# Two blocks over eight experts: the modulation row summed in four column groups, routing by scaled one-hots and bf16 counts, and one remainder moved ahead of the gate

## The reference

```python
# first block, mixture of experts
logits = (t @ w_router).astype(F32)
top_val, top_idx = lax.top_k(logits, TOP_K)          # TOP_K = 2, 8 experts
top_w = jax.nn.softmax(top_val, axis=-1)
combine = jnp.sum(jax.nn.one_hot(top_idx, N_EXPERTS, dtype=F32) * top_w[..., None], axis=1)
for e in range(N_EXPERTS):
    gt, up = jnp.split(t @ w_gate_up[e], 2, axis=-1)
    y = (jax.nn.silu(gt) * up) @ w_down[e]
    out = out + combine[:, e:e + 1].astype(t.dtype) * y
# second block, modulation row: (1, 1024) @ (1024, 6144)
ada = jax.nn.silu(c) @ w_ada[l] + b_ada[l]
shift_a, scale_a, gate_a, shift_m, scale_m, gate_m = jnp.split(ada, N_ADA, axis=-1)
```

## Time and profile before

| | |
|---|---|
| median of 3 runs | 1829.18 us (1827.13 to 1836.05) |
| the profiled execution | 1839.49 us, span 1837.7 us |
| mean granted TensorE clock | 0.981 |
| TensorE busy | 1782.2 us, 97% of the span |
| VectorE busy | 1412.2 us, 77% |
| ScalarE busy | 1113.0 us, 61% |
| GpSimd busy | 118.0 us, 6% |

### The profile page before, as it was taken

One profiled execution on the slowest core, in us unless ns is written; L12 is line 12 of the kernel. 1 busy time (PEld: TensorE's weight loads), 2 busy tenths in 40 slices (PEclk: granted clock), 3 DMA queues, 4 the chain that ended last, 5 costly groups with the idle time before them and its releaser, 6 DMA issues.

```text
span 1837.7 us, 22263 instructions
## 1 busy us (share of the span) xinstructions
PE 1782.2 (97%) x8380; PEld 1456.7 (79%) x8388; DVE 1412.2 (77%) x1225; ACT 1113.0 (61%) x1023; POOL 118.0 (6%) x147
## 2 busy tenths in 40 slices
PE   7979999999999999999999999999999989999998
PEld 6867788778777888888888888888888857778886
DVE  5556787858758888888888888888888976475556
ACT  5653444443537777777777777777777755543333
POOL 3010111112110000000000000000001010000000
PEclk9979999999999999999999999999999999999999
DMA  9536899744159999999999999999999984535550
GB/s 321 196 126 200 271 330 324 270 142 159 36 183 337 377 376 390 379 381 380 380 382 381 375 392 377 386 368 375 384 367 389 394 299 160 149 115 200 188 185 23
DMA packets 237227, 525.94 MB, mean 286 GB/s; under 512 B 16874, under 2 KB 40618, under 8 KB 236992
## 3 DMA queue, kind: packets, MB, share of 16 engines
q1 hardware_dynamic: 223376, 477.23, 72.2%
q0 software_dynamic: 13744, 47.32, 7.7%
HBM read 513.95 MB, written 10.53 MB: 285 GB/s over the span
## 4 chain that ended last, share of the span: by engine, by line
PE 91%; DVE 4%; ACT 2%; DMA 1%; issue 1%; DVEq 0%; SPq 0%; ACTq 0%
PE bank L2752 27%; PE bank L2753 27%; PE bank L2760 27%; PE bank L3192 1%; ACT w_hi L1029 1%; PE bank L2902 1%; DVE w_lo L1644 1%; PE bank L2864 1%; DMA raw<-in_moe_w_down 1%; DMA raw<-in_a_w_mem_kv 1%; PE bank L2808 1%; PE bank L2815 1%; PE bank L3074 0%; PE bank L3551 0%; PE bank L2854 0%
## 5 line engine op out<-in xcount | busy, mean ns | idle before, releaser
L1644 DVE TENSOR_TENSOR w_lo<-raw,w_hi 128x2048 fp32r<-128x2048 f32 x453 | 1040.6, 2300 | 224.4 <-ACT w_hi L1029 210.0
L1029 ACT ACTIVATE w_hi<-raw 128x2048 fp32r<-128x2048 f32 x453 | 867.2, 1916 | 480.3 <-PE bank L2753 341.4
L2752 PE MATMUL bank<-w_hi,slot_hi 128*128 128x512 f32 x896 | 357.1, 399 | 2.6 <-ACT w_hi L1029 2.6
L2753 PE MATMUL bank<-w_hi,slot_lo 128*128 128x512 f32 x896 | 351.0, 392 | 0.0
L2752 PE MATMUL bank<-w_hi,hT_hi 128*128 128x512 f32 (+1 forms) x704 | 279.2, 397 | 5.5 <-ACT w_hi L1029 3.2
L2753 PE MATMUL bank<-w_hi,hT_lo 128*128 128x512 f32 (+1 forms) x704 | 274.2, 390 | 0.0
L2760 PE MATMUL bank<-w_lo,slot_hi 128*128 128x512 f32 x896 | 240.6, 390 | 1.1 <-DVE w_lo L1644 1.1
L2752 PEld LDWEIGHTS bank<-w_hi,slot_hi 128*128 128x128 f32 x896 | 169.4, 189 | 36.6 <-issue 3.0
L2760 PEld LDWEIGHTS bank<-w_lo,slot_hi 128*128 128x128 f32 x896 | 168.1, 188 | 38.1 <-DVE w_lo L1644 2.8
L2753 PEld LDWEIGHTS bank<-w_hi,slot_lo 128*128 128x128 f32 x896 | 169.5, 189 | 33.5
L2760 PE MATMUL bank<-w_lo,hT_hi 128*128 128x512 f32 (+1 forms) x704 | 175.2, 391 | 0.0
(11 more groups left out here) (421 smaller groups left out, 1458.7 us busy)
## 6 DMA issues: line engine op xcount, KB each, us to landing
raw<-in_moe_w_gate_up SPq DMA_DIRECT2D x448, 512.0 KB, 5.9
raw<-in_moe_w_down SPq DMA_DIRECT2D x224, 512.0 KB, 5.8
raw<-in_w_ff SPq DMA_DIRECT2D x64, 512.0 KB, 4.4
work<-in_w_ada POOLq DMA_DIRECT2D x48, 512.0 KB, 5.5
raw<-in_dense_w_gate_up SPq DMA_DIRECT2D x44, 512.0 KB, 5.1
raw<-in_b_w_in SPq DMA_DIRECT2D x24, 512.0 KB, 5.1
raw<-in_w_in SPq DMA_DIRECT2D x24, 512.0 KB, 4.9
raw<-in_dense_w_down SPq DMA_DIRECT2D x22, 512.0 KB, 4.7
```

The source lines that it names most:

```text
L1029: act.activation(w_hi[:, g % SPLIT, 0:n], raw[:, g % RING, 0:n], ACT.Copy).then_inc(R.hi, 1)
L1644: dve.tensor_tensor(w_lo[:, g % SPLIT, 0:n], raw[:, g % RING, 0:n], f32(w_hi[:, g % SPLIT, 0:n]), ALU.subtract).then_inc(R.lo, 1)
L2752: pe.matmul(out_, hi, w_hi[:, s, c:c + w], start=(start and n == 0), stop=False, skip_group_check=True)
L2753: mm = pe.matmul(out_, lo, w_hi[:, s, c:c + w], start=False, stop=False, skip_group_check=True)
```

## The change

The twelve sums of the modulation row go to four groups of 32 columns: sum j fills partitions 32 (j mod 4) on, and three turns replace twelve rows. Four are made before `turn_first` and eight behind the first unit of `b_in`. The row's place is widened to all partitions, cleared by POOL, loaded with the bias in four transfers and stored in four. In the routing, POOL makes x times gain into `mix`, and the norm's scale moves into the one-hots of expert 0; ScalarE makes the scaled h for `h_dram` in `y_rows`. The marks of the chosen, the triangle, the ones, the token numbers and the one-hots of the seven other experts are bf16. ScalarE makes `w_hi` of the fifth unit ahead of the first Silu, VectorE its `w_lo` ahead of the first hidden product, and `route_rest` moves from ahead of the first step of `pair` to its end. The sizes of `one_row` and of a filler buffer (`even`) change with it; waits for the store count four transfers.

```diff
--- before.py
+++ after.py
@@ -59,6 +59,8 @@
 N_ADA = 6
+QUADS = 4
+ADA_TURNS = 2 * N_ADA // QUADS
 ADA_BUFFERS = 3
...
@@ -187,9 +189,10 @@
         zero = sb("zero", [P, P], BF16)
-        ones = sb("ones", [P, P])
+        exact = sb("exact", [P, 2 * P], BF16)
+        later_bf, ones_bf = exact[:, 0:P], exact[:, P:2 * P]
         c_col = sb("c_col", [P, KC])
-        one_row = sb("one_row", [P, 4 * N_ADA - 1])
+        one_row = sb("one_row", [P, 32 + ADA_TURNS - 1])
         sumsq = sb("sumsq", [P, TILES])
...
@@ -597,6 +602,7 @@
         pick = taken_a
+        pick_bf = [taken_a[:, t, P:P + (EXPERTS - 1) * P // 2].bitcast(BF16) for t in range(TILES)]
         h_again = rows[:, :, :]
...
@@ -662,7 +668,15 @@
-            return work[0:2 * N_ADA, 9216:9728]
+            return work[:, 9216:9728]
+
+        def ada_rows_of(quad):
+
+            return work[32 * quad:32 * quad + ADA_TURNS, 9216:9728]
+
+        def by_quad(rows):
+
+            return rows.rearrange("(r q) n -> q r n", q=QUADS)
...
@@ -674,14 +688,19 @@
             pool.wait_ge(*at("mix_a"))
-            pool.dma_start(ada_place(), A["b_ada_2"].rearrange("l (a n) -> (l a) n", n=512)).then_inc(ada_bias_in, 16)
+            pool.memset(ada_place(), 0.0).then_inc(ada_cleared, 1)
+            pool.wait_ge(ada_cleared, 1)
+            for quad in range(QUADS):
+                pool.dma_start(ada_rows_of(quad), by_quad(A["b_ada_2"].rearrange("l (a n) -> (l a) n", n=512))[quad])\
+                    .then_inc(ada_bias_in, 16)
             for n in range(ADA_ROWS):
...
             pool.wait_ge(*at("ada", "row"))
-            pool.dma_start(ada_dram, ada_place()).then_inc(ada_stored, 16)
+            for quad in range(QUADS):
+                pool.dma_start(by_quad(ada_dram)[quad], ada_rows_of(quad)).then_inc(ada_stored, 16)
...
@@ -916,8 +935,14 @@
                 load_gain()
+                pool.wait_ge(gain_in[0], 32)
+                pool.wait_ge(*at("b_out", "added", 1))
+                for t in range(TILES):
+                    o = pool.tensor_tensor(mix[:, t, :], x[:, t, :], gain[:, 0, :], ALU.mult)
+                o.then_inc(S("moe", "gained"), 1)
+                S.also("gain used", 2)
                 pool.wait_ge(*at("norm_moe", "h"))
-                pool.dma_start(h_dram.rearrange("(t p) d -> p t d", p=P), mix[:, :, :]).then_inc(h_stored, 16)
+                pool.dma_start(h_dram.rearrange("(t p) d -> p t d", p=P), y_rows[:, :, :]).then_inc(h_stored, 16)
             if have("ada"):
...
@@ -1293,7 +1318,7 @@
                     if j == 1 and have("ada"):
-                        act.wait_ge(ada_stored, 16)
+                        act.wait_ge(ada_stored, 16 * QUADS)
                     for h in range(2):
...
@@ -1339,10 +1364,14 @@
                 gained(2)
-                squares("moe", x, mix[:, 0, :], at("b_out", "added", 1))
+                squares("moe", x, y_rows[:, 0, :], at("b_out", "added", 1))
                 deviation("moe")
...
                 act.activation(ratio[:, 1, :], ratio[:, 0, :], ACT.Exp).then_inc(S("route", "exp"), 1)
+                act.wait_ge(*at("moe", "gained"))
+                for t in range(TILES):
+                    h = act.activation(y_rows[:, t, :], mix[:, t, :], ACT.Copy, scale=scale_col("moe", t))
+                h.then_inc(S("norm_moe", "h"), 1)
             if have("experts"):
...
@@ -1397,8 +1426,8 @@
                         split_hi(R, g + 3, 0)
+                        split_hi(R, FIRST_STEP, 0)
                         silu(0, g + 3, 0, 1)
-                        split_hi(R, FIRST_STEP, 0)
                         split_hi(R, FIRST_STEP + 1, 0)
...
@@ -1974,6 +2003,11 @@
                         dve.wait_ge(loaded["con"], 16)
+                        dve.tensor_copy(later_bf, con[:, C_LATER:C_LATER + P])
+                        for t in range(TILES):
+                            number = C_DIST + (TILES - 1 - t) * SEQ
+                            o = dve.tensor_copy(token_bf[:, t:t + 1], con[:, number:number + 1])
+                        o.then_inc(S("exact numbers"), 1)
                     if j in (2, 3):
...
@@ -2052,9 +2086,9 @@
                 if have("ada"):
-                    dve.wait_ge(ada_bias_in, 16)
+                    dve.wait_ge(ada_bias_in, 16 * QUADS)
                     dve.wait_ge(*at("ada", "summed"))
-                    dve.tensor_tensor(ada_place(), ada_place(), bank[2][0:2 * N_ADA, :], ALU.add).then_inc(S("ada", "row"), 1)
+                    dve.tensor_tensor(ada_place(), ada_place(), bank[2][:, :], ALU.add).then_inc(S("ada", "row"), 1)
...
@@ -2179,15 +2213,9 @@
                 dve.wait_ge(*S.last())
-                dve.tensor_scalar(chosen[:, :, :], rank[:, :, :], 1.5, None, ALU.is_lt).then_inc(S("route", "chosen"), 1)
+                dve.tensor_scalar(chosen[:, :, 0:EXPERTS], rank[:, :, :], 1.5, None, ALU.is_lt).then_inc(S("route", "chosen"), 1)
                 dve.tensor_scalar(seats[:, :, :], rank[:, :, :], 1.5, 1000.0, ALU.is_gt, ALU.mult).then_inc(S(), 1)
                 dve.wait_ge(*S.last())
-                g = gain_row(2)
-                for t in range(TILES):
-                    h = dve.scalar_tensor_tensor(out=mix[:, t, :], in0=x[:, t, :], scalar=scale_col("moe", t), in1=g,
-                                                 op0=ALU.mult, op1=ALU.mult)
-                h.then_inc(S("norm_moe", "h"), 1)
-                S.also("gain used", 2)
                 dve.wait_ge(*at("route", "order"))
...
@@ -2265,7 +2293,11 @@
                         for t in range(TILES):
-                            o = dve.tensor_scalar(pick[:, t, 0:P], iota, place[:, again, t, bass.ds(e, 1)], None, ALU.is_equal)
+                            if again:
+                                o = dve.tensor_scalar(pick[:, t, 0:P], iota, place[:, 1, t, bass.ds(e, 1)], None, ALU.is_equal)
+                            else:
+                                o = dve.tensor_scalar(pick[:, t, 0:P], iota, place[:, 0, t, e:e + 1], scale_col("moe", t),
+                                                      ALU.is_equal, ALU.mult)
                         o.then_inc(L.picked, 1)
...
@@ -2280,7 +2312,7 @@
                         for t in range(TILES):
-                            o = dve.tensor_tensor(pick[:, t, P:EXPERTS * P].rearrange("p (e s) -> p e s", e=EXPERTS - 1),
+                            o = dve.tensor_tensor(pick_bf[t].rearrange("p (e s) -> p e s", e=EXPERTS - 1),
                                                   iota.unsqueeze(1).broadcast_to([P, EXPERTS - 1, P]),
...
@@ -2296,15 +2328,16 @@
                         split_lo(R, g + 3, 0)
+                        split_lo(R, FIRST_STEP, 0)
                         hidden(0, 1)
-                        route_rest()
...
                             p, half, step = j % 2, j // EXPERT_STEPS, j % EXPERT_STEPS
-                            split_lo(R, g, r)
+                            if again or d > 0 or j > 0:
+                                split_lo(R, g, r)
                             if last and j == PAIR_STEPS - 1:
...
@@ -2323,6 +2356,8 @@
                             hidden(1 - p, n + 1)
+                            if not again and d == 0 and j == 0:
+                                route_rest()
                             if last and j == 8 and not again:
...
@@ -3071,8 +3106,10 @@
                     for j in range(first, last):
-                        mm = pe.matmul(bank[2][0:2 * N_ADA, :], one_row[:, 2 * N_ADA - 1 - j:4 * N_ADA - 1 - j],
-                                       work[:, j * 512:(j + 1) * 512], start=(j == 0), stop=(j == 2 * N_ADA - 1), skip_group_check=True)
+                        quad, turn_ = j % QUADS, j // QUADS
+                        mm = pe.matmul(bank[2][32 * quad:32 * quad + 32, :], one_row[:, ADA_TURNS - 1 - turn_:ADA_TURNS + 31 - turn_],
+                                       work[:, j * 512:(j + 1) * 512], start=(turn_ == 0), stop=(turn_ == ADA_TURNS - 1),
+                                       skip_group_check=True)
                     if last == 2 * N_ADA:
...
@@ -3088,10 +3125,8 @@
                     pe.wait_ge(ada_ready, ADA_ROWS)
-                    sum_ada(0, 2)
+                    sum_ada(0, QUADS)
                 turn_first()
-                if have("ada"):
-                    sum_ada(2, 4)
...
@@ -3118,7 +3153,7 @@
                         if (j, h) == (0, 0) and have("ada"):
-                            sum_ada(4, 2 * N_ADA)
+                            sum_ada(QUADS, 2 * N_ADA)
                         inside(j, h)
...
@@ -3171,10 +3206,10 @@
                 pe.wait_ge(*at("zero"))
-                later = con[:, C_LATER:C_LATER + P]
-                for c, terms in enumerate((((later, 0),), ((ones[:, :], 0), (later, 1)), ((ones[:, :], 0), (ones[:, :], 1)))):
+                pe.wait_ge(*at("exact numbers"))
+                for c, terms in enumerate((((later_bf, 0),), ((ones_bf, 0), (later_bf, 1)), ((ones_bf, 0), (ones_bf, 1)))):
```

(7 more changed lines are left out.)

20 lines of the change are left out of this document (11 added, 9 removed).

## The result

The changed kernel takes 1822.55 us in the median of six runs (1820.13 to 1824.51), the kernel before in the same comparison 1834.84 us (1827.13 to 1836.74). The ratio is 0.9936 [0.9922, 0.995]: 11.7 us faster, by the interval 9.2 to 14.3; the two medians lie 12.3 us apart. The forecast of 1816 us is 6.6 us too low, and both parts of it err the same way: the base, the median of three runs, was 5.7 us too low, and the saving of 13.2 us was 0.9 us more than the 12.3 us between the medians. The time lies within the range of 1810 to 1823 by 0.45 us, and that is luck. What follows weighs the saving.

What follows compares the result with a forecast made beforehand. TensorE, with 91% of the chain, was taken to bound the kernel. Terms of -5.55, -1.4, -2.0, -1.6, -2.6, -1.7 and +0.9 gave -13.95 us; 13.2 was taken off the 1829.18 median: 1816 us, range 1810 to 1823.

Steps and rivals of the forecast that it cites:

- The four records removed at 364.65 lay inside that wait: nothing: Modulation row: the records taken out lay inside TensorE's wait for VectorE's `hT_lo`, so removing them changes nothing.
- the routing, -1.4: Routing: picks start earlier, so TensorE's first weight unit starts at 536.1 instead of 537.50, 1.4 us saved.
- the naming, -2.0: Naming of tokens: 14 bf16 records replace 28, saving 2.0 us, and the clock staying up saves 1.6 us more.
- Column groups, -5.55: Modulation row sums: four groups run at once; 5.1 us saved on the last eight, 0.45 on the first four.
- Remainder ahead of the gate, -2.6 and -1.7: Fifth expert unit: TensorE's wait for `w_hi` goes, 2.6 us, and the unit takes 2.75 us instead of 4.41.
- `route_rest`, +0.9: Eleventh unit: the moved instructions stand before VectorE's `w_lo`, so TensorE waits about 0.9 us (bounds 0 and 1.7).
- (a): Whole kernel: the forecast itself holds, 1812 to 1819 us; chance 0.60.
- (b): Naming and first unit: the clock terms don't come back; gain 10.6 us, 1818 to 1820; chance 0.14.
- (c): Routing: POOL gets ahead of VectorE at 521.17, router's last columns 2.3 us later; gain 11.6, about 1818; chance 0.12.
- (d): Modulation row: groups don't overlap, or the bias or slack fails; gain 8.8 us, 1820.5; chance 0.05.
- (e): Fifth unit: TensorE waits for ScalarE anyway, on a load; gain about 9.6 us, 1819.5; chance 0.06.
- (f): Routing: POOL's product is late for TensorE; the kernel slower than before, 1830 to 1835 us; chance 0.03.

Runs made afterwards that it cites:

- the second profile: The kernel before, unchanged, profiled once more for a second execution: 1837.17 us.
- experiments 2 and 3: Changed kernel with column groups undone (1855.35 us; 1827.22 us with later buffers kept in place); separately, with the fifth unit's remainder back behind the gate (1824.61 us).
- experiment 5: Changed kernel with GpSimd's work made twice as long by two more products of the same size ahead of its own: 1824.45 us, ratio 0.9943.

## Which steps of the prediction held, and which failed

**The steps that failed.** The first is "The median of the runs is 1829.18 ... I take off 13.2": three runs stood for the kernel before, and five comparisons put its median at 1834.45 to 1835.62 us. That is 5.7 of the 6.6 us by which 1816 was missed. The second is a term put at nothing, "The four records removed at 364.65 lay inside that wait: nothing": TensorE stands 2.49 us there, and the clock fell behind that wait in the profiled execution, for 1.61 us. Two more terms of the sum were mis-sized: the routing, -1.4 and measured -2.39, and the naming, -2.0 and measured -2.84. The other terms held, and the sum of all was near what the traces show.

**Column groups, -5.55.** Held: 7.04 became 1.92 where 1.94 was worked out from the 1.07 us of the earlier trace rows; the sums start to start shrink by 5.12, the hT chain by 0.52 where 0.45 was taken, together -5.64 in executions without a fall. That GpSimd is not late held: four stores take 2.00 us and land by 376.53, its next product comes at 409.50. The four records removed at 364.65 were not nothing: without them TensorE is idle for 2.49 us, which cost 1.61 us of clock in the profiled execution and as much in one more of ten.

**Routing, -1.4: measured -2.39** (first unit 17.76 us behind the router's first product before, 15.37 now). Three pieces were mis-sized. The charge of 0.4 for GpSimd's lock was 0: POOL was free 0.06 us ahead of the first instruction with two SBUF inputs. The order's five records in bf16 take 0.28 us from the first start to the last end; that puts them some 0.03 apart, an estimate, not 0.06 to 0.11. The scaled picks take 0.60 us, 0.12 more where 0.2 was added. What sets the start is VectorE's chain, as written, and TensorE waits 0.91 for its end. The 2.39 us are made up so: the picks start 2.06 us sooner behind the router's first product, and from them to the first unit it is 0.33 us less.

**Naming, -2.0 and -1.6 of clock: -2.84 and -1.64.** From its first record to the next unit it takes 532.32 - 531.96 = 0.36 us, 0.026 for a product: both bounds for the spacing were too high, as they came from records of 8 columns in fp32 and half of that. One column in bf16 is cheaper than either. The Trainium skill ("TensorE: Matmul & The Clock Gate", "Weight-path perf modes") pointed the right way: by its figure the distance would have been near 0.06, and this case measured less than half of that. The run with fp32 names gives the pair back: 4.3 us in the trace, with the clock at 0.75, and 3.0 in the medians.

**Remainder ahead of the gate, -2.6 and -1.7: -2.58 and -1.69**, `w_hi` of the fifth unit read by TensorE at 537.85 with no wait. How much of that is clock depends on the naming: with the gate first and bf16 names the unit behind the wait began at full clock and still took 3.80 us. **`route_rest`, +0.9:** the wait is 0.75, the step of six units takes 558.51 - 540.57 = 17.94 us where it took 16.82, the stretch to the last `e_hid` by 0.8.

**The sum.** -5.64 - 11.1 + 0.8 = -15.9 us between profiled executions with no fall in the modulation row, -14.3 with it, against -13.95 predicted. The medians lie 12.3 and 13.6 us apart, the ratios give 11.7 and 12.5. Where the missing 1 to 4 us are isn't shown. That the profiled executions of before (1839.49 and 1837.17 us) lie 2 to 5 above its median of about 1835 is no more than the spread of executions. The prediction found "why is not visible"; the traces show where such differences arise, in the clock ahead of the sums, which moves their start by up to 10 us. The falls at the naming and at the fifth unit, 3.3 us, are too small for it: the fastest run of before, 1825.93 us, had a mean clock of 0.994 against 0.983 in the second profile, which had both, and 0.011 of 1835 us is six times 3.3.

**Rivals.** (a) happened by its mechanism, but not by its number: 1822.55 is 3.6 us above its 1812 to 1819, for the base. (b) is out: the clock terms came back (-3.3 us), though the mechanism it feared showed at another wait. (c): POOL came after VectorE's squares, 512.51 to 512.39; a price of that kind is real, and was paid in experiment 5. By the Trainium skill, "SBUF — State Buffer", "Who interferes with whom", the lock holds for the whole instruction: experiment 5 agrees, 2.31 us for 0.21. (d) and (e) are out by experiments 2 and 3, (f) by 518.15 against the 521.63 at which TensorE needs the product.

## What to carry to other kernels

Before calling an edit's neighbour unchanged, look at where its buffers start: 32 B in a buffer that nothing uses cost 27 us, twice what this change saves. A removed instruction that "lay inside a wait" is free only if the clock does not fall without it; here it fell in two executions of ten. Where two engines share SBUF, ask not only how long the new instruction is but which instruction of the other stands next to it: GpSimd's products ended 0.06 us ahead of the chain and cost nothing, and 4.6 us more of them cost 4.6 us. And take the base of a forecast from more than three runs where single runs spread by more than 10 us.

## What the runs showed of the hardware that was not expected

An fp32r product of 512 columns follows the one before by 0.2267 us when its stationary tile starts at 128 modulo 256 B in the partition (161152 and 161408, and `hT_hi` at 114816), and by some 0.233 us at 160, 192 or 0 (4.6 to 5.5 ns more for each of the 4008 on average). The addresses are those of the built programs. The rounded weights that stream past start at 128 modulo 256 as well (65664 and 82048); whether the residue itself counts or that both agree was not tried, and why it matters is open. First to last `e_hid` by the start of `slot_hi`: 929.9 us at 161152, 951.4 at 161184, 952.1 at 161216, 948.4 at 161280, 930.4 at 161408.
